# In a float32 network kernel on one core, the order of the wide and the narrow product in each chunk of the feed-forward matmuls, with one reversed pair per network

## What is computed

```python
def _conv_ffn(xn, w_up, conv_w, conv_b, w_down):      # (the second block's: silu, causal conv)
    a, gval = jnp.split(xn @ w_up, 2, axis=-1)        # 1024 -> 2 x 2816
    a = lax.conv_general_dilated(a, conv_w[:, None, :], ...) + conv_b
    return (jax.nn.gelu(a) * gval) @ w_down           # 2816 -> 1024
```

## Time and profile before

| | |
|---|---|
| device time, median of 3 runs | 1501.7 us |
| span of the profiled execution | 1500.4 us |
| TensorE busy (matmul) | 1482.2 us, 99% |
| TensorE weight loads | 1354.8 us, 90% |
| VectorE busy | 1106.1 us, 74% |
| ScalarE busy | 776.8 us, 52% |
| GpSimd busy | 488.6 us, 33% |
| TensorE on the chain that ended last | 95% |
| granted TensorE clock, mean | 0.998 of full |

### The profile page before, as it was taken

How to read it: one execution, slowest core, us unless ns; L and a number is a source line. 1 busy time by engine, 2 the same in 40 slices (tenths; PEclk the granted TensorE clock), 3 DMA queues, 4 the chain that set the end, 5 groups by cost and what they waited for, 6 DMA issues and landing times.

```text
span 1500.4 us, 24840 instructions
## 1 busy us (share of the span) xinstructions
PE 1482.2 (99%) x10662; PEld 1354.8 (90%) x10662; DVE 1106.1 (74%) x1156; ACT 776.8 (52%) x888; POOL 488.6 (33%) x295
## 2 busy tenths in 40 slices
PE   9999999999999999999999999999999998999997
PEld 7999999888888999999888889988888898988886
DVE  7747666788777557666888567978987568788853
ACT  6433544765544334444755456356664445665632
POOL 2306200245698408001254734002444000135410
PEclk9999999999999999999999999999999999999999
DMA  7674344555566563366555444334555534355552
GB/s 277 227 212 182 137 173 172 193 178 188 183 213 235 178 244 141 141 245 239 183 182 197 155 166 158 142 113 169 197 180 175 198 126 143 141 174 192 189 183 77
DMA packets 48589, 270.01 MB, mean 180 GB/s; under 512 B 11488, under 2 KB 14816, under 8 KB 19552
## 3 DMA queue, kind: packets, MB, share of 16 engines
q1 hardware_dynamic: 48480, 268.43, 50.8%
HBM read 261.59 MB, written 6.82 MB: 179 GB/s over the span
## 4 chain that ended last, share of the span: by engine, by line
PE 95%; DVE 3%; ACT 1%; DMA 1%; issue 0%; SPq 0%; DVEq 0%; ACTq 0%
PE gemm L566 38%; PE gemm L595 33%; PE aux L595 16%; DVE w_lo L1440 1%; PE aux L617 1%; PE aux L566 1%; PE gemm L676 1%; DMA h<-in_x 1%; PE aux L793 0%; PE gemm L678 0%; PE aux L653 0%; PE aux L666 0%; PE gemm L993 0%; PE aux L658 0%; ACT w_hi L1055 0%; PE aux L802 0%
## 5 line engine op out<-in xcount | busy, mean ns | idle before, releaser
L1440 DVE TENSOR_TENSOR w_lo<-raw,w_hi 128x2048 fp32r<-128x2048 f32 (+3 forms) x246 | 574.0, 2336 | 182.9 <-ACT w_hi L1055 180.2
L1055 ACT ACTIVATE w_hi<-raw 128x2048 fp32r<-128x2048 f32 (+3 forms) x246 | 457.0, 1858 | 308.7 <-PE gemm L566 184.2
L566 PE MATMUL gemm<-x_two,w_hi 128*128 128x256 f32 x1952 | 355.1, 284 | 0.0
L566 PEld LDWEIGHTS gemm<-x_two,w_hi 128*128 128x128 f32 x1952 | 303.6, 191 | 0.6
L566 PE MATMUL gemm<-x_two,w_lo 128*128 128x256 f32 x976 | 276.1, 283 | 0.0
L595 PE MATMUL gemm<-x_two,w_hi 128*128 128x512 f32 x672 | 234.6, 399 | 0.0
L2145 POOL TENSOR_TENSOR tmp<-tmp 128x512 f32<-128x512 f32 x24 | 38.9, 1622 | 477.2 <-ACT tmp L1082 463.2
L566 PEld LDWEIGHTS gemm<-x_two,w_lo 128*128 128x128 f32 x976 | 186.3, 191 | 0.0
L595 PE MATMUL gemm<-y_two,w_hi 128*128 128x512 f32 x528 | 185.3, 396 | 0.0
L2267 POOL TENSOR_TENSOR cv<-cv,rstd 128x512 f32<-128x512 f32 x44 | 116.6, 2649 | 179.3 <-ACT cv L1135 179.3
L595 PE MATMUL gemm<-x_two,w_lo 128*128 128x256 f32 x672 | 174.9, 281 | 0.0
(11 more groups left out here) (382 smaller groups left out, 2745.7 us busy)
## 6 DMA issues: line engine op xcount, KB each, us to landing
raw<-in_weights SPq DMA_DIRECT2D x222, 1024.0 KB, 4.8
raw<-in_weights SPq DMA_DIRECT2D x16, 768.0 KB, 4.2
raw<-in_weights SPq DMA_DIRECT2D x8, 512.0 KB, 4.3
raw<-in_weights SPq DMA_DIRECT2D x4, 576.0 KB, 3.6
s_inputs<-s_made SPq DMA_DIRECT2D x1, 2048.0 KB, 8.7
s_outputs<-s_cw SPq DMA_DIRECT2D x1, 2048.0 KB, 11.8
s_v<-s_inputs SPq DMA_DIRECT2D x1, 2048.0 KB, 9.8
s_cw<-s_outputs SPq DMA_DIRECT2D x1, 2048.0 KB, 10.6
```

The costliest lines, as they stand in the source:

```text
L566: mm = pe.matmul(out, lhs, rhs, start=fresh and m == 0, stop=end and m == 2, skip_group_check=True)
L1055: me.give(act.activation(w_hi[i % SPL][:, 0:n], raw[i % RAW][:, 0:n], ACT.Copy), w_hi_ready)
L1440: me.give(v.tensor_tensor(w_lo[i % RAW][:, 0:n], raw[i % RAW][:, 0:n], w_hi[i % SPL][:, 0:n].bitcast(F32), ALU.subtract), w_lo_ready)
```

## The change

In `gemm_halves` every pair is now wide, then narrow, also in the chunks that close an accumulation. One pair per network is turned round instead: that of chunk k = 3 in the first tile of the network's second block (`turned=(0, 3)`, for j == 1). The closing flag is now set on both matmuls of a closing pair. No instruction is added or taken away.

```diff
-            def gemm_halves(i, both, chunks_at=()):
+            def gemm_halves(i, both, chunks_at=(), turned=None):
...
                 for part in parts:
-                    for off, _, pairs, c0, n, _ in b.tiles:
+                    for at, (off, _, pairs, c0, n, _) in enumerate(b.tiles):
                         for k in part:
                             wc, xc = pairs[k]
                             if xc in todo:
                                 me.take(*todo.pop(xc))
+                            fresh, end = b.start and k == 0, b.stop and k == len(pairs) - 1
                             wide = (dst[:, off:off + BANK], wh[:, wc, c0:c0 + P], both[:, xc, :, :])
                             half = (dst[:, off:off + S], wl[:, wc, c0:c0 + P], both[:, xc, 0, :])
-                            fresh, end = b.start and k == 0, b.stop and k == len(pairs) - 1
-                            for m, (out, lhs, rhs) in enumerate((half, wide) if end else (wide, half)):
-                                mm = pe.matmul(out, lhs, rhs, start=fresh and m == 0, stop=end and m == 1,
-                                               skip_group_check=True)
+                            for m, (out, lhs, rhs) in enumerate((half, wide) if (at, k) == turned else (wide, half)):
+                                mm = pe.matmul(out, lhs, rhs, start=fresh and m == 0, stop=end, skip_group_check=True)
...
                 for j in range(2 * PAIRS):
-                    gemm_halves(i + j, both, BY_PAIR if j == 0 else ())
+                    gemm_halves(i + j, both, BY_PAIR if j == 0 else (), (0, 3) if j == 1 else None)
```

## The result

The changed kernel takes 1505.18 us (median of 12 runs: eleven lie from 1504.51 to 1507.37, one took 3729.02, and nothing here says why) against 1501.96 us for the kernel before on the same chips, a ratio of 1.0021 with a 95% interval of 1.0013 to 1.0029: slower by 3.2 us. The forecast was 1492.6 us, range 1491.0 to 1497.0. The time is rival A's, 1504.8, but the place in which things went wrong is rival C's, in all four networks at once.

A forecast was written before the change was run, and what follows sets the result against it. TensorE's matmul starts were taken as the bound, so time is won only where they move closer. Terms -7.7, -1.25 and -0.1 sum to -9.05 us; span 1500.4 becomes 1491.35, with 1.3 around it 1492.6 us, range 1491.0 to 1497.0.

The forecast's parts named there:

- rival A: In the up blocks the switch doesn't take and networks stay slow to their end: +3.1 us, 1504.8 us; chance 0.09.
- rival C: Only some networks switch, or something leads back to slow: one network lost 1495.9 us, two 1499; chance 0.12.
- the two paces: In the networks, the same wide-narrow pair costs 0.353 us (slow) or 0.3467 us (fast).
- the rhythm of three: In the networks' slow pace wide matmuls start 0.36, 0.35, 0.35 us apart: one long pair, two short ones.
- the rule of the switch: Reversed pair behind the second short pair switches to fast, behind the long one not; from fast, back to slow.
- item 5: Block 0 of each network and the closing flags: slow before and after, 0.02 us at most, taken as 0.
- Item 1 and 2: Each network's block 1 from 5.83 to 5.77 us, blocks 2 to 21 from 112.80 to 110.94: -1.92, four networks -7.7.
- Item 3: Down parts of networks 0, 2 and 3: 61.44 to 61.02 us, -0.42 each, -1.25 for three.
- Item 4: Down part of network 1, restarted by mixer matmuls: block 0 gains 0.10 us, the other 160 pairs taken as 0.
- Supply: Up stage: VectorE's 4.99 us a block stays hidden under 5.55; if it became the bound, 1497 us, chance 0.02.
- B: Order sets nothing; the pace belongs to the place in the program (bank, buffer, block): 1501.7 us; chance 0.07.
- the rule beside it: Trainium skill's back-to-back gap, N/2.4 + 2.5 ns: 0.325 us a pair in either order, nothing from this change.

The follow-up runs named there:

- e8_forms: Changed kernel, all pairs plain except pairs 4 and 5 of block 1, mixed wide-wide-narrow-narrow in network 2, narrow-narrow-wide-wide in network 3: 1498.91 us.
- e2_ends0: Changed kernel, with block 0 of each network given back its two reversed closing pairs: 1495.92 us, ratio 0.996.
- e5_word: Changed kernel with five reversed pairs per network (4, 9, 15, 20, 26 from the start of block 1) instead of one: 1493.11 us, ratio 0.9938.
- e6_word_off: As e5_word, with the fifth reversed pair one earlier (25): 1505.12 us, ratio 1.002.

## Why the prediction was wrong

- What bounds the kernel, the two paces, the rhythm of three and the rule of the switch: right. Each later reversed pair did what that rule says of its place, given the start; e8_forms, which breaks the turn in other ways, it doesn't cover.
- The step that failed is where the new reversed pair falls: "so k = 2 is the second short one, and a reversed k = 3 stands just where the switch is". That was read from block 1 of the kernel before, in which block 0 ends in reversed pairs. The same change made these plain. I had the block under item 5, "block 0 is slow before and after", and asked what it costs, not what it hands on; that the four networks agreed spoke for a fixed start only as long as block 0 ended the same way. In the changed kernel the long pair was k = 2 in network 0 and k = 1 in the others, so that the reversed k = 3 stood behind a long or a first short pair: each network's up part lost 0.27 us instead of gaining 1.92, and the down parts of networks 0, 2 and 3 lost 0.76 each instead of gaining 0.42. e2_ends0, which restores those ends alone, makes k = 2 the second short pair again in three networks of four, and these three switch.
- "behind the same two sum matmuls" held as a description and not as a reason: they pass the rhythm on. It depends on the order ahead of them and, in networks 0 and 1, on a wait there to a hundredth of a microsecond.
- Item 1 and 2, the size of a switched network: forecast 1.24 + 1.06 + 3.47 and 110.94, in all 116.71 for blocks 1 to 21; measured 116.70 (e2_ends0). Item 3: forecast 61.02 to the next start, measured 60.90 + 0.12. Item 4: forecast -0.1; the down part of network 1 takes 69.67 us to the next start in e2_ends0 against 69.86 before, but 69.69 in the changed kernel too, where nothing switched, so that this 0.2 isn't the fast pace's. Sum forecast -9.05, measured with all four switched -9.2 us (1493.11 against 1502.29).
- Supply: right. VectorE did 104.5 to 105.1 us of work in 116.8 us, and every up block behind block 2 of e5_word took 5.55 us.
- The rivals: A's arithmetic (+3.1) met the result (+3.2), with a cause that the runs refute. B and the rule beside it are refuted by e6_word_off against e5_word, the same matmuls and 12 us apart. C named the shifted start and gave it 0.12, priced as one network or two; what shifted was the start of all four, as each begins with a block 0 that the change altered.
- "The prediction is wrong if the up blocks show 5.65 us": block 6 of the changed kernel takes that.

## What to carry to other kernels

Where matmuls of two sizes take turns without a break, as here, the price of one can depend on the order of those well before it; measure starts over tens of matmuls, and look whether two stretches of the same instructions run at two paces. A fix that needs a certain place in such a rhythm has to be aimed with the trace of the changed program, not the one before, and holds only if nothing ahead of it waits by chance; a short sequence that brings every start to one state is sturdier. Runs that spread over several microseconds, in steps, can be a sign that a kernel has such states.

## What the runs showed of the hardware that was not expected

- Plain pairs of a 512-column and a 256-column matmul have two lasting paces here, 0.3467 and 0.3533 us a pair, over hundreds of pairs (116.70 against 118.90 us for 336 pairs), at the same granted clock.
- The pace passes over block edges, bank changes and fulfilled waits, and even the two float32 sum matmuls don't erase the place in the rhythm: 0.699 or 0.700 us at the place described above goes with a long pair k = 1 in 18 starts of 18.
- Behind a wait a network can come up in either pace by itself (three of the 18 starts of networks 0 and 1 above were fast).
- Why the slow pace has a period of three pairs, and what a break of the turn does to it, stays open. The rows of the weight loads don't tell: in both paces they are mostly 0.19 us long and begin some 0.003 us behind the start of a matmul.
